# Hybrid encoder with 32 experts on one core: rows of the last four experts kept in SBUF, the rest read back inside the loop

## The chip, the cores and the metric

The kernel runs on one core of a Trainium2 chip, as one launch. The metric is the time of that launch in microseconds; the median of three runs before the change is 1280.09 (1280.09 to 1281.01). The core has TensorE (PE, matmuls into PSUM), VectorE (DVE), ScalarE (ACT), GpSimd (POOL) and SyncE (SP, which here only issues transfers), and 16 DMA engines.

## The reference

Two layers over 512 tokens of 1024 float32 channels. Layer 0 mixes tokens with windowed attention, layer 1 with a gated DeltaNet that runs in both directions. Each ends with a mixture of experts, which is what the change touches:

```python
g_prob, g_idx = lax.top_k(jax.nn.softmax(g_logits, axis=-1), 1)      # 1 of 4 groups
e_prob, e_idx = lax.top_k(jax.nn.softmax(e_sel, axis=-1), TOP_K)     # 2 of its 8 experts
gate = g_prob * e_prob / jnp.sum(e_prob, axis=-1, keepdims=True)
expert_id = g_idx * EXPERTS_PER_GROUP + e_idx
combine = jnp.sum(jax.nn.one_hot(expert_id, N_EXPERTS, dtype=jnp.float32) * gate[..., None], axis=1)
hid = jax.nn.silu(jnp.einsum('td,edf->tef', t, w_gate)) * jnp.einsum('td,edf->tef', t, w_up)
hid = hid * combine[..., None].astype(hid.dtype)
return jnp.einsum('tef,efd->td', hid, w_down).reshape(B, S, D)
```

Every token so has two experts; x = x + (that sum) ends the layer. An expert is three matrices of 1 MB (gate, up: 1024 x 256; down: 256 x 1024), so one layer's 32 experts are 96 MB, read once each.

## The kernel before

Each engine has one instruction stream, written out by hand; semaphores join them. The order within a stream is the order of the code, so an instruction that waits holds up all that follows on its engine. There is no planner.

*Routing.* After the token mixer, `route_pe` and `moe_dve` find each token's two experts and its rank among an expert's tokens (`rank_f`). An expert has 64 slots (SLOTS). `idx_i[:, 0, e]` lists the token of each slot of expert e, `idx_i[:, 1, e]` the row of `y_rows` that each slot's result goes to. Where an expert had more than 64 tokens, `late_passes` would do the rest; every engine tests for it once in a layer, and it was not entered. `pick_rows` makes the rows of experts 0 and 1 with one-hot products; VectorE and ScalarE copy them out of PSUM (L1298, L1213), and the first transpose (`turn`, L1124) follows.

*The expert loop*, for e from 0 to 31. GpSimd gathers the rows of expert e + 4 from `h_rows` (L995). TensorE multiplies them by gate and up (`gate_and_up`, L1132), turns the next expert's rows (L1124), multiplies the hidden rows of expert e - 1 by its down matrix (`down_rows`, L1141, into bank 3: 64 slots x 1024 columns stand as two halves of 128 partitions), and turns the hidden rows of e (L1185). ScalarE computes silu (L1224) and copies turned rows (L1217). VectorE multiplies silu by up (L1323), copies the output of e - 1 to `y_out` (`take_y`, L1319) and the turned hidden rows of e (L1328). GpSimd scatters `y_out` to `y_rows` in DRAM, at row (choice k, token) (`scatter`, L1002).

*Weights.* SP issues the loads of all weights in order (`load_gate_up` L2382, `load_down` L2388) into 7 homes for gate and up and 8 for down, each as soon as TensorE has used its former content. One of these homes is x itself: x is written to `x_rows` before the loop and read again behind the last weights (L2428). For layer 1's token mixer, a first panel of 2 MB (L2373) follows in the same queue.

*The tail of layer 0.* When all scatters have landed, SP reads `y_rows` back as two rows of 1024 for each token (`read_back`, L1392, 8 transfers of 512 KB) into `y_in` in the arena. VectorE, which has meanwhile split the low part of the first panel (`split_low`, L174; ScalarE the high part, L168), adds gate times row to x (`combine_best` L1348, `combine_second` L1353), normalises (`norm_dve`, L285 and L288) and turns; the first projection of the DeltaNet begins on TensorE (`first_unit_half`, L150). Spare matmuls (`spare_pe`, L1092) fill TensorE's time in places.

*The tail of layer 1.* `send_out` reads back in the same way (L1377), `finish_dve` adds (L1363), and each tile of x is stored to the output (L1383).

## Time and profile before

| | us |
|---|---|
| median of 3 runs | 1280.09 |
| the profiled execution | 1278.82 |
| its span on the core | 1277.1 |
| TensorE busy | 1145.1 (90%) |
| VectorE busy | 519.5 (41%) |
| ScalarE busy | 383.5 (30%) |
| GpSimd busy | 385.5 (30%) |
| read from and written to HBM | 265.83 MB and 27.26 MB |

The first expert loop runs from about 251 to 492, the second from about 1012 to 1255. A row of the page cuts the span into 40 slices and gives a digit for each: the busy share in tenths. In a timeline, each line is one or several like instructions: start, length, engine, line of the code, operation, output<-inputs, count, and in brackets how long the engine was idle before it and what ended that. "SPq" is the issuing of transfers, not their run. A row of --windows gives for each engine its busy time and its instructions. A row of a group by form gives busy time and mean ns of one behind the first bar.

### The profile page before, as it was taken

Reading aid. Unit: us, or ns where it says so; the run is one execution under the profiler, and the core shown is the slowest. Engines: PE = TensorE matmul, PEld = TensorE weight load, DVE = VectorE, ACT = ScalarE, POOL = GpSimd, SP = SyncE. Lnnn points to the kernel's source line nnn. Section 1 sums busy time; section 2 is a strip of 40 time slices with the busy share of each in tenths; the row PEclk is TensorE's granted clock in tenths of the full one; section 3 lists DMA queues with packets and bytes.
Section 4 is the critical chain, followed back from the end, with each engine's and each line's share of the span. In section 5 each row is a group of like instructions: output and inputs, shape, how many; then the busy total and the mean of one; then the engine's idle time right before and its main releaser. Section 6 shows DMA issues by size and latency. Waiting matters only on the chain.

```text
span 1277.1 us, 21577 instructions
## 1 busy us (share of the span) xinstructions
PE 1145.1 (90%) x8755; PEld 805.1 (63%) x8755; DVE 519.5 (41%) x1188; ACT 383.5 (30%) x854; POOL 385.5 (30%) x428
## 2 busy tenths in 40 slices
PE   5999999899999884989889999889999899999782
PEld 4876678655555442868568887678888555555441
DVE  4466663411111114564684455753653411111114
ACT  3426841111111102354553445543422111111010
POOL 1233621112232211047545266542301022322110
PEclk9999999999999997989999999999999899999896
DMA  7121047999999998111000120002366999999996
GB/s 241 67 73 67 2 192 277 368 364 381 383 386 379 383 392 320 69 66 67 2 3 1 67 101 31 3 2 81 151 247 261 359 372 389 388 386 377 380 390 247
DMA packets 67795, 278.24 MB, mean 218 GB/s; under 512 B 16888, under 2 KB 16984, under 8 KB 43120
## 3 DMA queue, kind: packets, MB, share of 16 engines
q1 hardware_dynamic: 56480, 255.89, 52.7%
q0 software_dynamic: 11072, 20.43, 4.7%
q8 instruction: 72, 1.18, 0.4%
q10 hardware_dynamic: 144, 0.52, 0.1%
q14 instruction: 27, 0.22, 0.1%
HBM read 265.83 MB, written 27.26 MB: 230 GB/s over the span
## 4 chain that ended last, share of the span: by engine, by line
PE 69%; DMA 13%; DVE 8%; ACT 4%; SPq 3%; issue 2%; POOL 1%; DVEq 0%; POOLq 0%
PE bank L1132 14%; PE bank L150 9%; PE bank L152 8%; PE bank L151 8%; DMA hn<-in_moe_w_up 8%; PE bank L1141 6%; PE bank L1676 4%; PE bank L1124 3%; DMA x<-in_moe_w_up 3%; SPq L2382 2%; PE bank L541 2%; PE bank L550 1%; PE bank L575 1%; PE bank L389 1%; PE bank L298 1%
## 5 line engine op out<-in xcount | busy, mean ns | idle before, releaser
L1002 POOL DMA_INDIRECT y_rows<-arena,idx_i x64 | 64.5, 1008 | 350.0 <-DVE arena L1319 345.0
L1224 ACT ACTIVATE arena<-bank 128x128 f32<-128x128 f32 x64 | 17.7, 277 | 368.2 <-PE bank L1132 368.2
L1323 DVE TENSOR_TENSOR arena<-arena,bank 128x128 f32<-128x128 f32 x64 | 18.4, 287 | 259.2 <-ACT arena L1224 259.2
L152 PE MATMUL bank<-ring_r,ht_r 128*128 128x512 f32 x288 | 113.0, 392 | 0.0
L1132 PE MATMUL bank<-ring,arena 128*64 128x256 f32 x832 | 101.6, 396 | 7.7 <-DMA ring<-in_moe_w_up 6.7
L1319 DVE COPY arena<-bank 128x512 f32<-128x512 f32 x64 | 44.2, 691 | 144.2 <-PE bank L1141 144.2
L150 PE MATMUL bank<-ring_r,arena_r 128*128 128x512 f32 (+1 forms) x228 | 91.3, 401 | 6.1 <-DVE ring_r L174 5.4
L151 PE MATMUL bank<-ring_r,arena_r 128*128 128x512 f32 x224 | 87.8, 392 | 0.0
L1132 PEld LDWEIGHTS bank<-ring,arena 128*64 128x64 f32 x832 | 57.9, 136 | 42.7 <-DMA ring<-in_moe_w_up 7.7
L151 PE MATMUL bank<-ht_r,ring_r 128*128 128x512 f32 (+1 forms) x224 | 80.9, 361 | 0.0
L1124 PEld LDWEIGHTS bank<-ident,arena 64*128 64x128 f32 x512 | 61.3, 201 | 28.3 <-issue 25.1
L995 POOL DMA_INDIRECT arena<-h_rows,idx_i x60 | 57.1, 951 | 66.7 <-issue 36.4
L174 POOL TENSOR_TENSOR ring_r<-ring,ring_r 128x1024 fp32r<-128x1024 f32 x32 | 75.8, 2389 | 2.7 <-ACT ring_r L168 2.7
L2173 DVE SCALAR_TENSOR_TENSOR arena<-bank,arena 128x511 f32<-128x511 f32 (+1 forms) x72 | 53.9, 749 | 51.0 <-ACT arena L1870 49.3
L1124 PE MATMUL bank<-ident,arena 64*128 64x64 f32 x512 | 70.0, 277 | 1.6 <-DVE arena L1298 1.6
L152 PEld LDWEIGHTS bank<-ring_r,ht_r 128*128 128x128 f32 x288 | 54.3, 189 | 11.6
L150 PE MATMUL bank<-ring_r 128*128 128x512 f32 (+1 forms) x144 | 55.8, 387 | 3.3 <-DVE hn L2364 2.0
L168 ACT CAST ring_r<-ring 128x1024 fp32r<-128x1024 f32 x52 | 52.1, 1047 | 9.3 <-DMA ring<-in_gdn_w_in 6.0
L150 PEld LDWEIGHTS bank<-ring_r,arena_r 128*128 128x128 f32 (+1 forms) x228 | 42.9, 188 | 17.8 <-ACT arena_r L305 4.9
L1217 ACT COPY arena<-bank 128x512 f32<-128x512 f32 x64 | 37.4, 585 | 48.2 <-PE bank L1124 48.2
L1132 PE MATMUL bank<-arena 128*64 128x256 f32 x320 | 43.2, 427 | 6.3 <-DMA arena<-in_moe_w_up 4.8
L1676 PE MATMUL bank<-arena,ring 128*128 128x128 f32 x352 | 45.6, 291 | 3.6 <-POOL ring L2049 2.9
(343 smaller groups left out, 2338.4 us busy)
## 6 DMA issues: line engine op xcount, KB each, us to landing
ring<-in_moe_w_gate SPq DMA_DIRECT2D x26, 1024.0 KB, 21.5
ring<-in_moe_w_up SPq DMA_DIRECT2D x26, 1024.0 KB, 25.3
arena<-in_moe_w_down SPq DMA_DIRECT2D x24, 1024.0 KB, 27.5
ring<-in_moe_w_down SPq DMA_DIRECT2D x24, 1024.0 KB, 26.9
ring<-in_gdn_w_in SPq DMA_DIRECT2D x8, 2048.0 KB, 8.0
arena<-in_moe_w_gate SPq DMA_DIRECT2D x10, 1024.0 KB, 19.4
arena<-in_moe_w_up SPq DMA_DIRECT2D x10, 1024.0 KB, 23.3
ht<-in_moe_w_gate SPq DMA_DIRECT2D x10, 1024.0 KB, 27.0
```

The costliest lines, as they stand in the source:

```text
L150: pe.matmul(dst, a[0], b[0], start=start, stop=False)
L151: pe.matmul(dst, a[0], b[1], start=False, stop=False)
L152: return pe.matmul(dst, a[1], b[0], start=False, stop=stop)
L168: act.copy(panel(n, True, True)[:, c, :], panel(n)[:, c, :]).then_inc(panel_high, 1)
L174: eng.tensor_tensor(panel(n, False, True)[:, c, :], panel(n)[:, c, :], panel(n, True, True)[:, c, :].bitcast(F32), ALU.subtract).then_inc( ...
L995: pool.indirect_dma_start(out=rows_of(e), out_offset=None, in_=h_rows[l], in_offset=bass.IndirectOffsetOnAxis(ap=idx_i[0:SLOTS, 0, e:e + 1 ...
L1002: pool.indirect_dma_start(out=y_rows[l], out_offset=bass.IndirectOffsetOnAxis(ap=idx_i[:, 1, e:e + 1], axis=0), in_=y_out[:, e % RING, :], ...
L1124: last = pe.transpose(bank[0][:, c * SLOTS:(c + 1) * SLOTS], rows_of(e)[:, c::KC], ident[at, at])
L1132: last = pe.matmul(bank[1][m * SLOTS:(m + 1) * SLOTS, 0:2 * P].rearrange("p (w n) -> p w n", w=2), xgt[:, i, c * SLOTS:(c + 1) * SLOTS], w ...
L1141: last = pe.matmul(bank[3][half * SLOTS:(half + 1) * SLOTS, :], hidden_t[:, i, m * SLOTS:(m + 1) * SLOTS], d[:, m, half * HALF:(half + 1) ...
L1676: last = pe.matmul(bank[b][:, h * P:(h + 1) * P], lhs(h), rhs(h), start=True, stop=True)
L2173: last = dve.scalar_tensor_tensor(out=acc, in0=bank[U % 4][:, of], scalar=tap(k, unit), in1=acc, op0=ALU.mult, op1=ALU.add)
```

## The change

The outputs of experts 28 to 31 (`SENT` to 31) are not scattered. VectorE multiplies them by the slot's gate while it takes them out of PSUM (`keep_y`), two experts to a pair of 128-partition tiles, odd experts with their halves changed over. ScalarE and VectorE split each into a rounded high part and a low part (`kept_high`, `kept_low`). Where a token's row stands in a pair is marked by one-hot matrices (`mark_slots`, `turn_marks`, `spread_of`), and TensorE adds the rows of both pairs for each half tile of 512 columns in one PSUM bank (`kept_pair`), which VectorE adds to x (`add_kept_dve`). The gates of the slots come from eight small products ahead of the loop (`gates_to_slots`); the operations that compute the gates move ahead of the loop's first copy.

The other rows are still scattered and read back. The read-back stands behind the x tiles in SP's stream and waits for expert 28's output. Its homes are the down homes 1 to 4. Tiles 0 and 1 are added by VectorE, tile 0 between experts 30 and 31 and behind expert 31, tile 1 behind the loop; tiles 2 and 3 are scaled by ScalarE (`scale_rows`) and added by GpSimd. Both layers now have the same tail. Rows of `y_rows` that no one writes any more are multiplied by a gate of 0; so that they hold numbers, both `y_rows` are filled with x during the attention (`fill_rows`, 16 writes). The second panel of the DeltaNet's projection waits for all additions, and TensorE for all of x.

Left out below: the places of new buffers and counts of semaphores, the late passes (which are not entered), and the small operations on gates.

```diff
+KEPT = 4
+SENT = EXPERTS - KEPT
...
-        y_in = [cut(2 * D * t, 2, D) for t in range(TT)]
+        y_in = [dn_home[1 + t].rearrange("p (k n) -> p k n", k=2) for t in range(TT)]
+        y_late = [gu_home[4 + t // 2][:, t % 2 * 2 * D:(t % 2 + 1) * 2 * D].rearrange("p (k n) -> p k n", k=2)
+                  for t in range(TT)]
...
+            for e in range(SENT):
                 if e + AHEAD < EXPERTS:
                     gather(e + AHEAD)
                 scatter(e)
+            pool.wait_ge(x_again, Y_FILLED + 16 * TT * (l + 1))
+            for t in (2, 3):
+                for k in range(2):
+                    pool.wait_ge(s["exp_g"], 6 + 2 * (t - 2) + k + l * PER["exp_g"])
+                    last = pool.tensor_tensor(x[:, t, :], x[:, t, :], y_in[t][:, k, :], ALU.add)
+                    if k == 0 or t == 2:
+                        o.step(last)
+            last.then_inc(s["idx"], 1)
...
-            def down_rows(i, slot):
+            def down_rows(i, slot, turned_halves=0):
                 d = down(slot)
                 for m in range(FC):
                     for half in range(2):
-                        last = pe.matmul(bank[3][half * SLOTS:(half + 1) * SLOTS, :],
+                        side = half ^ turned_halves
...
+            def gates_to_slots():
+                pe.wait_ge(s["onehots"], 2 + l * PER["onehots"])
+                for n in range(2 * TT):
+                    last = pe.matmul(bank[2][:, 2 * EXPERTS:2 * EXPERTS + KEPT], at_slot[:, n // TT, n % TT, :],
+                                     last_gate[:, n, :], start=n == 0, stop=n == 2 * TT - 1)
+                last.then_inc(s["ranks"], 1)
+
+            def turn_marks():
+                pe.wait_ge(s["onehots"], 3 + l * PER["onehots"])
+                for q in range(2):
+                    for ab in range(2):
+                        for t in range(TT):
+                            last = pe.matmul(bank[4 + 2 * q + ab][:, t * P:(t + 1) * P],
+                                             marks_of(q, t)[:, ab * SLOTS:ab * SLOTS + P], unit_r,
+                                             start=True, stop=True)
+                        last.then_inc(s["ranks"], 1)
+
+            def kept_pair(q, n):
+                t, ab = n // 2, n % 2
+                for high in (True, False):
+                    if n < 2:
+                        if high:
+                            pe.wait_ge(s["exp_e"], 2 + 2 * q + ab + l * PER["exp_e"])
+                        else:
+                            pe.wait_ge(s["dve"], 3 + 2 * q + ab + l * PER["dve"])
+                    last = pe.matmul(bank[(4 + n) % 8][:, :], spread_of(q, ab)[:, t * P:(t + 1) * P],
+                                     kept_y(q, ab, high), start=q == 0 and high, stop=q == 1 and not high)
+                return last
+
+            def add_kept():
+                pe.wait_ge(s["exp_g"], 5 + l * PER["exp_g"])
+                pe.wait_ge(s["xgt"], EXPERTS * (l + 1))
+                pe.wait_ge(s["hidden"], EXPERTS * (l + 1))
+                pe.wait_ge(s["hid_t"], EXPERTS * (l + 1))
+                for n in range(2 * TT - 1):
+                    kept_pair(0, n)
+                pe.wait_ge(s["y_copied"], EXPERTS * (l + 1))
+                kept_pair(0, 2 * TT - 1)
+                for n in range(2 * TT):
+                    kept_pair(1, n).then_inc(s["lists"], 1)
...
+            gates_to_slots()
             turn(0)
             for e in range(EXPERTS):
                 body(e)
+                if e == SENT - 1:
+                    turn_marks()
             project_down(EXPERTS - 1)
             late_passes(pe, l, None, late)
+            add_kept()
...
+            def scale_rows(t):
+                act.wait_ge(y_back[t], 16 + 32 * (l + 1))
+                for k in range(2):
+                    act.activation(y_in[t][:, k, :], y_in[t][:, k, :], ACT.Copy, scale=stat[:, 10 + k, t:t + 1]
+                                   ).then_inc(s["exp_g"], 1)
+
+            def kept_high(q):
+                act.wait_ge(s["placed"], 2 * TT + 1 + q + l * PER["placed"])
+                act.copy(kept_y(q, 0, True), kept_y(q, 0, False, False)).then_inc(s["exp_e"], 1)
+                act.wait_ge(s["y_copied"], SENT + 2 * q + 2 + l * PER["y_copied"])
+                act.copy(kept_y(q, 1, True), kept_y(q, 1, False, False)).then_inc(s["exp_e"], 1)
...
+                if e == SENT:
+                    for n in range(4):
+                        act.wait_ge(s["ranks"], 3 + n + l * PER["ranks"])
+                        act.copy(spread_of(n // 2, n % 2), bank[4 + n][:, :]).then_inc(s["exp_g"], 1)
+                if e == SENT + 2:
+                    kept_high(0)
+            scale_rows(2)
+            kept_high(1)
+            scale_rows(3)
...
+            def keep_y(e):
+                q, odd_one = (e - SENT) // 2, e % 2
+                dve.wait_ge(s["y_sum"], e + 1 + l * PER["y_sum"])
+                for ab in range(2):
+                    at = slice(SLOTS * (ab ^ odd_one), SLOTS * ((ab ^ odd_one) + 1))
+                    last = dve.tensor_scalar(kept_y(q, ab, False, False)[at, :], bank[3][at, :],
+                                             slot_gate[at, e - SENT:e - SENT + 1], None, ALU.mult)
+                    if odd_one and ab == 0:
+                        last.then_inc(s["placed"], 1)
+                last.then_inc(s["y_copied"], 1)
+
+            def kept_low(q):
+                for ab in range(2):
+                    dve.wait_ge(s["exp_e"], 2 + 2 * q + ab + l * PER["exp_e"])
+                    dve.tensor_tensor(kept_y(q, ab, False), kept_y(q, ab, False, False),
+                                      kept_y(q, ab, True).bitcast(F32), ALU.subtract).then_inc(s["dve"], 1)
+
+            def mark_slots():
+                numbers = slot_no[:, 0:SLOTS].unsqueeze(1).unsqueeze(1)
+                for q in range(2):
+                    marks = flat_ring[True][:, 2 * PAIR + q * 3 * TT * SLOTS:2 * PAIR + (q + 1) * 3 * TT * SLOTS]
+                    marks = marks.rearrange("p (t w n) -> p t w n", t=TT, w=3)
+                    for w, n in ((0, 2), (2, 1)):
+                        first = 2 * q + w % 2
+                        dve.tensor_tensor(marks[:, :, w:w + n, :], numbers.to_broadcast([P, TT, n, SLOTS]),
+                                          last_slot[:, :, first:first + n].unsqueeze(3).to_broadcast([P, TT, n, SLOTS]),
+                                          ALU.is_equal)
+                dve.tensor_copy(unit_r, ident[:, :]).then_inc(s["onehots"], 1)
...
+                if e > SENT:
+                    keep_y(e - 1)
+                elif e:
                     take_y(e - 1)
                 dve.wait_ge(s["hid_turned"], e + 1 + l * PER["hid_turned"])
                 dve.tensor_copy(hidden_t[:, e % RING, :], bank[2][:, 0:P]).then_inc(s["hid_t"], 1)
-            take_y(EXPERTS - 1)
+                if e == SENT - 2:
+                    mark_slots()
+                if e == SENT + 2:
+                    kept_low(0)
+                    combine_rows(dve, l, 0, 0, o)
+                if e == SENT + 3:
+                    combine_rows(dve, l, 0, 1, o)
+            keep_y(EXPERTS - 1)
+            kept_low(1)
...
+            combine_rows(dve, l, 1, 0, o)
+            combine_rows(dve, l, 1, 1, o)
+            for t in range(TT):
+                add_kept_dve(dve, l, t)
...
+        def combine_rows(dve, l, t, k, o):
+            if k == 0:
+                dve.wait_ge(x_again, Y_FILLED + 16 * TT * (l + 1))
+                dve.wait_ge(y_back[t], 16 + 32 * (l + 1))
+            o.step(dve.scalar_tensor_tensor(out=x[:, t, :], in0=y_in[t][:, k, :], scalar=stat[:, 10 + k, t:t + 1],
+                                            in1=x[:, t, :], op0=ALU.mult, op1=ALU.add))
+
+        def add_kept_dve(dve, l, t):
+            if t == 2:
+                dve.wait_ge(s["idx"], 2 + l * PER["idx"])
+            for half in range(2):
+                n = 2 * t + half
+                c = slice(half * HALF, (half + 1) * HALF)
+                dve.wait_ge(s["lists"], 2 + n + l * PER["lists"])
+                dve.tensor_tensor(x[:, t, c], bank[(4 + n) % 8][:, :], x[:, t, c], ALU.add
+                                  ).then_inc(s["combined"], 1)
...
+        def fill_rows(sp):
+            for l in range(2):
+                whole = y_rows[l].rearrange("(r h) n -> r (h n)", h=2)
+                for n in range(2 * TT):
+                    sp.dma_start(whole[n * P:(n + 1) * P, :], x[:, n % TT, :]).then_inc(x_again, 16)
...
+            sp.wait_ge(s["ranks"], PER["ranks"] * (l + 1))
+            sp.wait_ge(s["y_sum"], SENT + 1 + l * PER["y_sum"])
...
+            read_back(sp, l)
...
+            fill_rows(sp)
...
-            used = [(s["up"], 27), (s["y_sum"], 32)] + [(g["proj"], 4), (g["proj"], 8), (g["av"], 8), (g["proj"], 16)]
+            used = [(s["up"], 27), (s["combined"], 2 * TT)] + [(g["proj"], 4), (g["proj"], 8), (g["av"], 8), (g["proj"], 16)]
...
-                if i == 0:
-                    read_back(sp, 0)
...
+            pe.wait_ge(s["combined"], 2 * TT)
...
-            for t in range(2):
-                combine_best(dve, t, o)
-                combine_second(dve, t)
```

## Rows read from the trace of the kernel before

**Rows 1.** The page, the span in 40 slices of 31.9 us.

```profile
...
DMA  7121047999999998111000120002366999999996
...
```

**Rows 2.** Timeline, end of the first expert loop (start, length, engine, line, [idle before]).

```profile
...
483.60 3.85 PE L1132 MATMUL bank<-hn,arena 128*64 128x256 f32 x32 [0.82 <-DMA hn<-in_moe_w_up]
...
487.80 0.29 DVE L1323 TENSOR_TENSOR arena<-arena,bank 128x128 f32<-128x128 f32 x1 [4.35 <-ACT arena L1224]
...
490.20 1.94 PE L1141 MATMUL bank<-arena 128*64 128x512 f32 x8 [0.78 <-DVE arena L1328]
...
498.55 3.88 ACT L168 CAST ring_r<-ring 128x1024 fp32r<-128x1024 f32 x4 [5.97 <-DMA ring<-in_gdn_w_in]
...
499.62 4.63 DVE L174 TENSOR_TENSOR ring_r<-ring,ring_r 128x1024 fp32r<-128x1024 f32 x4 [5.90 <-ACT ring_r L168]
...
506.82 4.76 PE L1092 MATMUL bank<-router,ones 128*128 128x288 f32 x12 [14.69 <-DVE x L1353]
...
510.05 0.15 DVE L285 TENSOR_SCALAR norm_s<-norm_s 128x1 f32<-128x1 f32 x1
...
518.15 0.36 PE L150 MATMUL bank<-ring_r 128*128 128x256 f32 x1 [1.30 <-DVE ht_r L318]
...
```

**Rows 3.** One line's instruction and landing: last x tile read again, first layer.

```profile
...
L2428 SPq DMA_DIRECT2D x<-x_rows x1: 6911/6911/6911, 467.6 to 467.6; - x1
...
DMA to landing us min/median/max: 25.0/25.0/25.0
```

**Rows 4.** The same for the last x tile of the second layer.

```profile
...
L2428 SPq DMA_DIRECT2D x<-x_rows x1: 2762/2762/2762, 1230.8 to 1230.8; - x1
...
DMA to landing us min/median/max: 23.4/23.4/23.4
```

**Rows 5.** Windows (PE, PEld, DVE, ACT, POOL busy; granted clock; DMA share; GB/s).

```profile
...
496.00:498.00 2.00, 0.00 (x0) 0.00 (x0) 0.00 (x0) 0.00 (x0) 0.00 (x0) 0.60 0.16 64
508.00:510.00 2.00, 2.00 (x6) 1.43 (x5) 1.96 (x2) 0.00 (x0) 0.00 (x0) 0.50 1.03 414
510.00:512.00 2.00, 1.59 (x7) 0.92 (x5) 1.32 (x3) 1.15 (x2) 0.56 (x1) 0.99 1.02 398
...
```

**Rows 6.** Timeline, last expert and tail of the second layer.

```profile
...
1246.17 3.85 PE L1132 MATMUL bank<-hn,arena 128*64 128x256 f32 x32 [0.93 <-DMA hn<-in_moe_w_up]
...
1250.38 0.29 DVE L1323 TENSOR_TENSOR arena<-arena,bank 128x128 f32<-128x128 f32 x1 [4.46 <-ACT arena L1224]
...
1252.77 1.94 PE L1141 MATMUL bank<-arena 128*64 128x512 f32 x8 [0.78 <-DVE arena L1328]
...
1262.44 10.26 DVE L1363 SCALAR_TENSOR_TENSOR x<-arena,x 128x1024 f32<-128x1024 f32 x9 [7.00 <-DMA arena<-y_rows]
1268.86 4.66 SPq L1383 DMA_DIRECT2D out<-x  x5
```

**Rows 7.** Timeline, start of the first expert loop.

```profile
...
240.93 1.90 PE L1117 MATMUL bank<-arena 128*128 128x64 f32 x16
...
250.76 0.69 DVE L1298 COPY arena<-bank 128x512 f32<-128x512 f32 x1 [7.48 <-PE bank L1152]
...
251.50 0.76 PE L1124 MATMUL bank<-ident,arena 64*128 64x64 f32 x5 [0.79 <-DVE arena L1298]
...
```

**Rows 8.** Groups by form on VectorE: costs of one operation.

```profile
...
L1363 DVE SCALAR_TENSOR_TENSOR x<-arena,x 128x1024 f32<-128x1024 f32 x7 | 8.8, 1284 | 7.1 <-DMA arena<-y_rows 7.0
...
L406 DVE TENSOR_TENSOR x<-x,bank 128x512 f32<-128x512 f32 x16 | 11.0, 687 | 40.0 <-PE bank L152 40.0
...
```

**Rows 9.** Groups by form on ScalarE.

```profile
...
L1217 ACT COPY arena<-bank 128x512 f32<-128x512 f32 x64 | 37.4, 585 | 48.2 <-PE bank L1124 48.2
...
L271 ACT ACTIVATE hn<-x 128x1024 f32<-128x1024 f32 x16 | 16.9, 1058 | 87.7 <-DVE x L406 72.3 <-DVE x L1353 11.0 <-DMA x<-in_x 4.1
...
```

**Rows 10.** Groups by form on GpSimd.

```profile
...
L174 POOL TENSOR_TENSOR ring_r<-ring,ring_r 128x1024 fp32r<-128x1024 f32 x32 | 75.8, 2389 | 2.7 <-ACT ring_r L168 2.7
...
L2121 POOL TENSOR_TENSOR ring<-arena 128x512 f32<-128x512 f32 x12 | 12.2, 1039 | 2.0 <-PE bank L1676 2.0
...
```

140 lines of the change are left out of this document (80 added, 60 removed).

## The prediction

> **What bounds the kernel now.** I read the DMA row of the page first: its share is 9 tenths or more through both expert loops and near zero in most of what lies before each [rows 1]. Read next to it the timeline at the end of the first loop: the last expert's gate and up product began at 483.60, when its weights landed, and that expert's output left TensorE at 492.14 (490.20 + 1.94). From there to 518.15, the first projection of the next layer, TensorE has no matmul that the output needs: 26.0 us for scattering, reading back, adding and normalising [rows 2]. So the loops end by DMA, and behind each is a tail in which VectorE and transfers take turns.
>
> The landings say when a transfer queued in the loop arrives. The last of the four x tiles read again was issued at 467.6 and landed 25.0 us later, at 492.6 [rows 3]; in the second layer at 1230.8 + 23.4 = 1254.2 [rows 4]. That is after the last expert's weights in both. The windows give the rate of plain 4 KB rows, 414 GB/s, so 1 MB of two row tiles takes 2.5 us and 4 MB 10.1 us; they also give TensorE's granted clock: idle since 492.14, it shows a mean of 0.60 in 496 to 498 and 0.50 (the 1.2 GHz level) in 508 to 510, although it works from 506.82; the next row has 0.99 [rows 5]. In the second layer the last product began at 1246.17, its hidden product ran at 1250.38, its output was done at 1254.71; the last output store was issued from 1268.86 on and the span ended at 1277.1 [rows 6].
>
> **The change, part by part.** All sums are against the profiled execution, 1278.82 us with a span of 1277.1; the median of the runs is 1280.09, 1.27 more, which I add at the end.
>
> *Fill of y_rows.* 16 writes of 512 KB, 8.4 MB, 20 us at 414 GB/s, are issued on SP behind the second attn_w_out load, issued at about 105. The DMA row is at zero in slices 5 of 128 to 160 us and nearly so around it, and SP's next load of expert weights waits until the attention ends [rows 1]. Price 0; without that cover 20 us.
>
> *Start of the expert loop.* Eight one-hot products with 4 columns stand between the picking of rows and the first transpose. The nearest row is the same number with 64 columns, 1.90 us; bounds 1.0 (weights alone, my estimate as half of it) and 1.9, I take 1.6. They begin when the picking ends, about 250.7, so the transpose begins at 252.3, not 251.50: +0.8. The some 16 small VectorE operations moved ahead fit in its 7.48 us of idle time there [rows 7]. TensorE frees the weight homes, so the loads shift with it, and DMA ends the loop: +0.8 in each layer, +1.6 in all (0 to 2.2).
>
> *In the loop.* The marks, their 16 transposes, four copies, and a second VectorE instruction for each kept tile (0.69 each, the price of 512 columns out of PSUM [rows 8]) meet one to three microseconds of waiting for weights per expert, as the 0.82 before 483.60. Price 0 up to expert 30. Four scatters fewer save only what lies ahead of the last weights, below 0.3 us.
>
> *The read-back moved inside.* This is the step that decides. SP asks for it once expert 28's output is there (about 474 and 1237), behind the x tiles in the same queue. VectorE waits for the first tile and for all four x tiles between experts 30 and 31, in its own stream. Behind that wait stand the hidden product of expert 31, the keeping of expert 30, the copy of the turned hidden rows; TensorE's last transpose and last down product wait for these, and ScalarE's splitting of the last pair waits in turn behind its own wait for tile 2. First tile in the first layer: between 492.6 (landed with x) and 495.1 (one tile behind), I take 494.0. Then:
>
> VectorE adds the first half of tile 0 (1.28 [rows 8], with its wait 1.3) to 495.3; hidden product to 495.6, against 487.8 before. Keeping expert 30 and the copy (2 x 0.65 + 0.3) to 497.2. TensorE has then been idle since its products of about 489.2, as it was from 492.14 ahead of the low row [rows 5], so I take the lower clock: the last down product costs 3.9 instead of 1.94, to 501.2. Keeping expert 31, to 502.6. ScalarE: tile 2 lands at 499.0, its two scalings (1.06 each) end at 501.1, the two roundings (0.59 each [rows 9]) at 503.2. The low part to 503.9, the test for late passes 0.4, tile 1's two additions to 506.9. The one-hot products, 32 of 512 columns at 0.24 (eight passes in 1.94), run ahead of that, from 501.6 to 509.3. VectorE then takes eight half tiles out of PSUM at 0.61 from start to start (0.69 long): 511.8. GpSimd's four additions: 1024 columns cost 2.39 in one row and 2 x 1.04 in another [rows 10]; at 2.1 from 500.1 they end at 508.5, just ahead of VectorE's need at 509.3.
>
> Now comes what VectorE formerly did while it waited: the low split of the first projection panel, 4.63 from 499.62, and 0.42 for the gate weights. The panel is itself queued behind 4 MB: formerly landed at 498.55, now 508.6 if all 10.1 us come on top, and some 504.9 (my estimate) if part of it fits into DMA share that lay idle before (0.16 was busy in 496 to 498, which alone gives 1.7); I take 506.6, which ScalarE's split turns into 507.6. So VectorE goes on to 516.9. From its first normalising instruction to the first projection took 8.1 us (510.05 to 518.15); the addition in the middle is gone, I take 7.6: 524.5. First layer: +6.3. Its bounds: with the early landings and the higher clock 521.1, +3.0; with the late ones and 2.39 on GpSimd 525.9, +7.8. TensorE's work behind that point is unbroken before and stays so.
>
> Second layer by the same steps: first tile between 1254.2 less what idle DMA share gives (1252) and 1256.7, I take 1255.5; hidden product to 1257.1 against 1250.7; last output, at the lower clock, 1262.7; kept 1264.1, split 1265.4, tile 1 1268.4, eight additions 1273.4. The end follows 4.4 behind the last addition (1262.44 + 10.26 = 1272.7, span end 1277.1 [rows 6]): 1277.8, +0.7. Bounds: -4.7 and +2.3.
>
> *Taken away.* Of 8 additions of 1024 columns behind each read-back two stay on VectorE behind the loop; 10.26 us become 2.6 + 4.9 [rows 6]. That gain is real, but it begins 8 and 6 us late.
>
> *Waits moved.* The second panel of the projection now waits for all additions (about 512 instead of 503) and lands near 520; it was split only from 538 on. TensorE's wait for all of x rather than for its first tile costs nothing: normalising is behind it anyway.
>
> Sum: 1.6 + 6.3 + 0.7 = +8.6: 1287.4 profiled, **1288.7** as a median. With every lower bound: 0 + 3.0 - 4.7 = -1.7, 1278.4; with every upper one 2.2 + 7.8 + 2.3 = +12.3, 1292.4.
>
> *A rule against the change.* The additions of tile 1 on VectorE read two operands of SBUF while GpSimd's do too. GpSimd's same-sized additions are 2.39 in one row and 2.08 in another, so some mutual hindrance is possible [rows 10]. The Trainium skill, SBUF — State Buffer, section "SBUF: two separate sides", says that the two share a port pair as "an exclusive lock, not a bandwidth split", for a VectorE operation with two SBUF inputs against a GpSimd one that reads SBUF. By that rule the forecast gains the price of the third rival below; without it the sum above stands. No row here shows the two engines' additions of this size side by side.
>
> *Order of landings.* The x tiles landed 25.0 and 23.4 us after their issue, behind weights issued before them [rows 3, 4]. The Trainium skill, DMA: Bandwidth & Descriptors, section "Queues, rings and completion order", says that descriptors of one issuing engine are consumed in ring order on each DMA engine, but that completion is not first in, first out. The first half speaks for the wait; the second allows single tiles to land early, which is the first rival.
>
> **Rivals.**
> 1. *The rows are there in time* (faster). One mechanism: the first tile lands before 487.5 and 1250.1, VectorE never waits, the clock holds. Then the second tail is 1254.7, kept 1256.1, split 1257.9, tile 1 1260.9, additions 1265.8, end 1270.3: -6.8. The first tail gains nothing: the panel behind 4 MB lands at 504.9 at the earliest, and 1.05 + 4.65 + 7.6 is 518.2. Sum -6.8 + 1.6: 1274.9 as a median. For it: transfers queued in one stream do not land in strict order. Against: the x tiles alone, waited for at the same place, landed at 492.6 and 1254.2.
> 2. *Landings at the lower bounds* (no change): the idle share of the DMA engines takes the read-back, the clock stays up: -1.7 to +1, some 1279.8. For it: the DMA share had fallen below 1 before the loop's end.
> 3. *GpSimd and VectorE exclude each other*: each of two additions of tile 1 waits up to 2.1 for GpSimd, whose last then ends 2.6 later; 2.6 to 4.2 in each layer on top of the sum, 1294.5.
> 4. *The change does not do what it says*: the rows are asked for inside the loop and arrive behind it. That is the forecast's own mechanism.
>
> **How the numbers follow.** Forecast 0.58, rival 1 0.12, rival 2 0.18, rival 3 0.12. The range takes in rival 2 and the upper bound: 1279 to 1294. What a measurement can tell is 0.2%, 2.6 us. Slower: the forecast, rival 3 and a small part of rival 2 make 0.71; rival 2's rest and the forecast's low edge 0.15; faster 0.14.
>
> **What would show it.** In the profile after: the hidden product of expert 31 idle until a read-back tile or x lands, some 6 to 8 us past the end of its gate and up product; TensorE's clock at 0.5 in the last down product; VectorE's low split of the panel behind the additions, the first projection 5 to 7 us later relative to the last weights; the first transpose about 1 us later. I am wrong if VectorE finds tile 0 landed, or if the first projection starts no later than before.

## The result, and the profile after

| | before | after |
|---|---|---|
| median of the runs, us | 1280.55 (4 runs, 1280.09 to 1281.83) | 1300.74 (4 runs, 1297.96 to 1302.20) |
| ratio, 95% interval | | 1.0153 (1.0133 to 1.0174) |
| the profiled execution, its span | 1278.82, 1277.1 | 1302.20, 1300.2 |

Slower, as forecast, but by 20 us instead of 8.6: the time is above the range of 1279 to 1294. The profiled execution is the slowest of the four, about 1.5 above their median; I come to that below.

I cut both spans at the same instructions: the last gate and up product of each layer, the first projection between them, and the end.

| stretch | before | after | difference | forecast |
|---|---|---|---|---|
| start to last gate and up product, layer 0 | 483.6 | 484.5 | +0.9 | +0.8 |
| from there to the first projection (first tail) | 34.6 | 47.6 | +13.1 | +6.3 |
| from there to the last gate and up product, layer 1 | 728.0 | 730.6 | +2.6 | +0.8 |
| from there to the end (second tail) | 30.9 | 37.4 | +6.5 | +0.7 |
| sum | | | +23.1 | +8.6 |

First tail in the profile after, by the timeline (start, length, engine, line); the rows answer to [rows 2].

```profile
...
484.50 3.85 PE L1172 MATMUL bank<-hn,arena 128*64 128x256 f32 x32 [0.44 <-DMA hn<-in_moe_w_up]
...
495.99 1.28 DVE L1528 SCALAR_TENSOR_TENSOR x<-ring,arena,x 128x1024 f32<-128x1024 f32 x1 [9.22 <-DMA ring<-y_rows]
497.31 0.29 DVE L1478 TENSOR_TENSOR arena<-arena,bank 128x128 f32<-128x128 f32 x1
...
497.66 0.47 PE L1226 MATMUL bank<-ident,arena 128*128 128x128 f32 x1 [7.60 <-DVE arena L1478]
...
499.45 3.68 PE L1182 MATMUL bank<-arena 128*64 128x512 f32 x8 [1.32 <-DVE arena L1485]
...
500.98 2.19 ACT L1308 ACTIVATE arena<-arena 128x1024 f32<-128x1024 f32 x2 [12.31 <-DMA arena<-y_rows]
...
502.27 5.37 POOL L1045 TENSOR_TENSOR x<-x,arena 128x1024 f32<-128x1024 f32 x2 [33.29 <-ACT arena L1308]
...
503.24 1.53 DVE L1452 TENSOR_SCALAR ring<-bank,slot_gate 64x512 f32<-64x512 f32 x2 [2.58 <-PE bank L1182]
...
504.69 3.50 DVE L1461 TENSOR_TENSOR ring_r<-ring,ring_r 128x512 fp32r<-128x512 f32 x2
...
507.72 6.02 POOL L1045 TENSOR_TENSOR x<-x,ring 128x1024 f32<-128x1024 f32 x2
508.12 6.71 DVE L1528 SCALAR_TENSOR_TENSOR x<-spare,arena,x 128x1024 f32<-128x1024 f32 x2
508.64 3.89 ACT L170 CAST ring_r<-ring 128x1024 fp32r<-128x1024 f32 x4 [0.83 <-DMA ring<-in_gdn_w_in]
514.86 4.88 DVE L1538 TENSOR_TENSOR x<-bank,x 128x512 f32<-128x512 f32 x8
...
519.99 4.62 DVE L176 TENSOR_TENSOR ring_r<-ring,ring_r 128x1024 fp32r<-128x1024 f32 x4
...
```

Read it from the top. VectorE stood 9.22 us until the second row of tile 0 had landed, and the hidden product of expert 31 (L1478) came at 497.31 instead of 487.80: the forecast's wait. TensorE had no work for 7.60 us, and the last down product took 3.68 instead of 1.94. Then look at the pairs that overlap: the two low parts (L1461), 0.68 each when alone, took 3.50 beside GpSimd's addition, and the two additions of tile 1 (L1528), 1.28 each when alone, 6.71. The eight additions out of PSUM (L1538) took what was forecast, 4.88.

The second tail, from the last hidden product on, answers to [rows 6].

```profile
...
1272.81 1.28 DVE L1528 SCALAR_TENSOR_TENSOR x<-ring,arena,x 128x1024 f32<-128x1024 f32 x1 [7.80 <-DMA ring<-y_rows]
...
1276.27 3.68 PE L1182 MATMUL bank<-arena 128*64 128x512 f32 x8 [1.32 <-DVE arena L1485]
...
1279.00 4.86 POOL L1045 TENSOR_TENSOR x<-x,arena 128x1024 f32<-128x1024 f32 x2 [30.99 <-ACT arena L1308]
...
1281.51 5.66 DVE L1461 TENSOR_TENSOR ring_r<-ring,ring_r 128x512 fp32r<-128x512 f32 x2
...
1283.94 5.46 POOL L1045 TENSOR_TENSOR x<-x,ring 128x1024 f32<-128x1024 f32 x2
...
1287.09 4.71 DVE L1528 SCALAR_TENSOR_TENSOR x<-spare,arena,x 128x1024 f32<-128x1024 f32 x2
...
1291.84 4.87 DVE L1538 TENSOR_TENSOR x<-bank,x 128x512 f32<-128x512 f32 x8
...
```

Here the low parts took 5.66 and tile 1's additions 4.71. The page after, in 40 slices of 32.5 us, has this DMA row for the one in [rows 1]: the fill is the 7 and 1 in slices 4 and 5, the rest is nearly the same.

```profile
...
DMA  7127157899999995111000121002366999999993
...
```

The start of the loop answers to [rows 7]: the gates' products took 1.84, against 1.6 forecast, and the transpose follows at 253.60. That is 2.1 later than before, not 0.8, because the picking ahead of it ended later in this execution (251.8 against 250.7); at the last gate and up product 0.9 of it was left.

```profile
...
251.83 1.84 PE L1231 MATMUL bank<-arena 128*128 128x4 f32 x16
...
253.60 1.09 PE L1164 MATMUL bank<-ident,arena 64*128 64x64 f32 x8
...
```

### The profile page after: what moved, and what is told of

Its sections match the earlier page's. It is cut to its first block, busy times and chain, and to the rows that moved or that the text cites. A ratio compares the mean times of both kernels' runs of the same rounds, so it can differ in the third digit from the quotient of the medians.

```text
span 1300.2 us, 21938 instructions
## 1 busy us (share of the span) xinstructions
PE 1176.4 (90%) x8883; PEld 830.3 (64%) x8883; DVE 550.3 (42%) x1243; ACT 400.7 (31%) x878; POOL 399.6 (31%) x428
## 4 chain that ended last, share of the span: by engine, by line
PE 67%; DMA 14%; DVE 9%; ACT 4%; SPq 3%; issue 2%; POOL 1%; DVEq 0%
PE bank L1172 12%; PE bank L152 9%; PE bank L154 8%; PE bank L153 8%; DMA ring<-in_moe_w_up 8%; PE bank L1182 6%; PE bank L1847 4%; PE bank L1164 3%; DMA ring<-y_rows 3%; DMA arena<-in_moe_w_up 2%; PE bank L546 2%; PE bank L555 1%; PE bank L580 1%; PE bank L300 1%; PE bank L392 1%
## 5 line engine op out<-in xcount | busy, mean ns | idle before, releaser
L1028 POOL DMA_INDIRECT y_rows<-arena,idx_i x56 | 57.2, 1021 | 301.6 <-DVE arena L1445 295.5
L1478 DVE TENSOR_TENSOR arena<-arena,bank 128x128 f32<-128x128 f32 x64 | 18.4, 288 | 243.0 <-ACT arena L1322 242.9
L1445 DVE COPY arena<-bank 128x512 f32<-128x512 f32 x56 | 38.7, 692 | 128.6 <-PE bank L1182 128.6
L154 PEld LDWEIGHTS bank<-ring_r,ht_r 128*128 128x128 f32 x288 | 54.6, 190 | 11.7
L152 PEld LDWEIGHTS bank<-ring_r,arena_r 128*128 128x128 f32 (+1 forms) x228 | 43.1, 189 | 17.1 <-ACT arena_r L307 4.9
L1303 ACT COPY arena<-bank 128x512 f32<-128x512 f32 x64 | 37.4, 585 | 49.9 <-PE bank L1164 49.9
L1182 PE MATMUL bank<-arena 128*64 128x512 f32 x192 | 50.0, 644 | 2.6 <-DVE arena L1485 2.6
L1226 PEld LDWEIGHTS bank<-ident,arena 128*128 128x128 f32 x64 | 9.0, 140 | 64.3 <-issue 48.7
```

What stands on the lines that cost most here:

```text
L152: pe.matmul(dst, a[0], b[0], start=start, stop=False)
L154: return pe.matmul(dst, a[1], b[0], start=False, stop=stop)
L1028: pool.indirect_dma_start(out=y_rows[l], out_offset=bass.IndirectOffsetOnAxis(ap=idx_i[:, 1, e:e + 1], axis=0), in_=y_out[:, e % RING, :], ...
L1182: last = pe.matmul(bank[3][side * SLOTS:(side + 1) * SLOTS, :], hidden_t[:, i, m * SLOTS:(m + 1) * SLOTS], d[:, m, half * HALF:(half + 1) ...
```

## The experiments

All times are medians; the kernel before was measured beside each (1279.7 to 1280.4) and ratios are against it. After is 1300.7.

### What GpSimd's additions cost

**In the kernel before, by itself.** Four additions of 1024 columns on GpSimd, read by nobody, beside VectorE's in the second tail:

```diff
...
             moe_pool(pool, 1, o)
+            pool.wait_ge(y_sent[0], Y_SENT[0] + 16)
+            for t in range(TT):
+                pool.tensor_tensor(hn[:, t, :], y_in[0][:, 0, :], y_in[0][:, 0, :], ALU.add)
```

> The kernel before, with four additions of 1024 columns on GpSimd (2.1 to 2.4 us each when alone), started when the first tile of the second layer has been read back, that is beside VectorE's eight of 1.28 us; their result is read by nobody. It measures by itself what GpSimd's additions do to VectorE's. Theory A (only one of the two engines has the port when both read two operands of SBUF): VectorE's additions beside them take up to 3.4 us, and the end comes 4 to 9 us later. Theory B (they share it with little loss): VectorE's stay at 1.28 to 1.6, the end comes under 1.5 us later, and what was slow in the kernel after has another cause.

Measured: 1283.94, ratio 1.0039 (1.0022 to 1.0056); span 1282.4 against 1277.1. First VectorE's groups by form while GpSimd worked (until 1272.6), then those behind it:

```profile
...
L1363 DVE SCALAR_TENSOR_TENSOR x<-arena,x 128x1024 f32<-128x1024 f32 x4 | 11.4, 2920 | 6.9 <-DMA arena<-y_rows 6.9
...
L1363 DVE SCALAR_TENSOR_TENSOR x<-arena,x 128x1024 f32<-128x1024 f32 x3 | 3.7, 1279 | 0.0
...
L2527 POOL TENSOR_TENSOR hn<-arena 128x1024 f32<-128x1024 f32 x4 | 10.4, 2625 | 5.1 <-DMA arena<-y_rows 5.1
...
```

The same operation took 2.92 us beside GpSimd's additions and 1.28 without them, four times in a row, one for each of GpSimd's. The engines take turns, a pair every 2.83 us. Theory A, by the lengths. The last addition ends 6.0 later (1278.73, formerly 1272.69) and the span is 5.3 longer; the median moved by 3.6 (2.8 to 7.2 by the interval), just under theory A's 4 and clear of theory B's 1.5.

**In the kernel after.** First in both layers:

```diff
-                    last = pool.tensor_tensor(x[:, t, :], x[:, t, :], y_in[t][:, k, :], ALU.add)
+                    last = pool.tensor_tensor(x[:, t, 0:32], x[:, t, 0:32], y_in[t][:, k, 0:32], ALU.add)
```

> The kernel after, with GpSimd's four additions of 1024 columns cut to 32 columns each: 992 of 1024 columns of the read-back rows of tiles 2 and 3 are left out of the result, and nothing else. The wait inside the loop and the slow last down product stay. VectorE's operations that took 0.68 and 1.28 us alone and up to 2.9 and 3.4 beside GpSimd's additions then have nothing beside them. Theory A (GpSimd's additions cost what the forecast missed): the last addition out of PSUM comes 6 us earlier in each layer (L0 at about 513.5 instead of 519.7, L1 6.5 earlier), and the time is 1300.7 - 12.5 = 1288, within 2 of the forecast of 1288.7. Theory B (the additions out of PSUM wait for the one-hot products or for the rows, whatever GpSimd does): under 6 us in all, 1295 or more.

Measured: 7487.59. The routing of the second layer hangs on the first layer's rows; an expert then had more than 64 tokens and the late passes ran, so this time says nothing. But the first tail of its trace lies ahead of that routing, and it is the first tail of the kernel after without GpSimd's additions:

```profile
...
504.56 1.46 DVE L1461 TENSOR_TENSOR ring_r<-ring,ring_r 128x512 fp32r<-128x512 f32 x2
506.91 2.61 DVE L1528 SCALAR_TENSOR_TENSOR x<-spare,arena,x 128x1024 f32<-128x1024 f32 x2 [0.90 <-issue]
509.55 4.87 DVE L1538 TENSOR_TENSOR x<-bank,x 128x512 f32<-128x512 f32 x8
...
526.80 0.36 PE L152 MATMUL bank<-ring_r 128*128 128x256 f32 x1 [0.79 <-DVE ht_r L320]
...
```

1.46 and 2.61 in place of 3.50 and 6.71. The last addition ends at 514.42, 5.3 earlier than in the kernel after (theory A had 6), and the tail, from the last gate and up product at 484.33 to the first projection, is 42.5, 5.1 shorter than after's 47.6. The wait for tile 0 (8.79 us) and the slow last product (3.68) are still in it.

With 32 columns in the second layer alone (`n = 32 if l else D`):

> The kernel after, with GpSimd's four additions cut to 32 of their 1024 columns in the second layer only, where no routing hangs on them: 992 of 1024 columns of the read-back rows of tiles 2 and 3 are left out of the second layer's result. The wait in the loop and the slow last down product stay, the first layer is whole. Theory A (GpSimd's additions cost what the forecast missed): in the second tail the two low parts and tile 1's additions take 0.68 and 1.28 us each instead of 2.89, 2.84 and 3.39, the last addition comes 6 to 6.5 us earlier relative to the last gate and up product (27.5 instead of 33.9 behind it), the tail from there to the end is 31 instead of 37.4, and the time 1294.5. Theory B (the additions out of PSUM wait for the one-hot products or for the rows, whatever GpSimd does): under 3 us, 1298 or more.

Measured: 1294.65, ratio 1.0116 (1.0085 to 1.0147). The second tail is 31.4 (1260.1 to 1291.5), 6.0 shorter than after's 37.4. VectorE in its timeline:

```profile
...
1278.88 1.45 DVE L1462 TENSOR_TENSOR ring_r<-ring,ring_r 128x512 fp32r<-128x512 f32 x2
1280.57 2.60 DVE L1529 SCALAR_TENSOR_TENSOR x<-spare,arena,x 128x1024 f32<-128x1024 f32 x2 [0.24 <-issue]
1283.21 4.87 DVE L1539 TENSOR_TENSOR x<-bank,x 128x512 f32<-128x512 f32 x8
...
```

1.45 and 2.60 in place of 5.66 and 4.71. The wait in the loop and the slow last product are still in this kernel, and its second tail of 31.4 is what I had forecast (31.6). So the second layer's miss is GpSimd's additions, shown; and of the first layer's 6.8 they are 5.1, by the trace above.

**GpSimd's share given to VectorE.** Tiles 2 and 3 added by VectorE; the scaling on ScalarE and GpSimd's additions are gone, and with them the waits for them (the cut shows ScalarE's and VectorE's streams):

```diff
...
-            scale_rows(2)
             kept_high(1)
-            scale_rows(3)
...
             combine_rows(dve, l, 1, 1, o)
+            for t in (2, 3):
+                combine_rows(dve, l, t, 0, o)
+                combine_rows(dve, l, t, 1, o)
```

> The changed kernel, but VectorE adds all four tiles itself; ScalarE scales nothing and GpSimd adds nothing; VectorE's wait inside the loop stays. Theory A (VectorE operations with two SBUF operands are blocked while GpSimd adds): the two low parts of the last pair take 1.3 us together instead of 3.5 and 5.7, the two additions of tile 1 take 2.6 instead of 6.7 and 4.7; what is saved pays for the four additions more on VectorE, 5.1 us: -2 us in all against the changed kernel. Theory B (these rows are long for another reason, the transfers that write SBUF or waits inside them): they stay as long, and the four additions come on top, +5 us in each layer, +10.

Measured: 1298.79, ratio 1.0146 (1.0110 to 1.0183); the first tail is as long as after's (47.7), the second 36.7 against 37.4. The low parts took 1.45 and tile 1's additions 2.61, as theory A had it. The medians are 2.0 apart, but the runs overlap (1298.36 to 1300.13 here, 1297.96 to 1302.20 after), so no difference can be told: four more additions of 1.30 in each layer on VectorE cost about what the turns with GpSimd did, and GpSimd's help gained nothing that these runs can tell.

### What the wait in the loop costs

**The wait moved behind the loop, nothing else.**

```diff
...
                     kept_low(0)
-                    combine_rows(dve, l, 0, 0, o)
-                if e == SENT + 3:
-                    combine_rows(dve, l, 0, 1, o)
...
             kept_low(1)
+            combine_rows(dve, l, 0, 0, o)
+            combine_rows(dve, l, 0, 1, o)
```

> The changed kernel, but VectorE adds tile 0 behind the loop, not between experts 30 and 31 and behind 31. Theory A (VectorE's wait for the first tile is what makes the tails late, as the prediction had it): the last down product ends some 9 us earlier in each layer and both tails end 7 to 8 us earlier, together -15 us against the changed kernel. Theory B (ScalarE, which waits for tile 2 ahead of its rounding of the last pair, holds the tail as late by itself): the last down product is 9 us earlier, but the low part of the last pair follows the landing of tile 2 and moves by 1 to 2 us in each layer, together -3 us.

Measured: 1306.23, ratio 1.0210 (1.0173 to 1.0248): 5.5 slower than after, no run of the one within the range of the other. Both theories expected a gain, and both fell. The expert's last output left TensorE at 492.2 instead of 503.1, and yet:

```profile
...
501.95 4.25 DVE L1461 TENSOR_TENSOR ring_r<-ring,ring_r 128x512 fp32r<-128x512 f32 x2 [8.15 <-ACT ring_r L1313]
506.13 6.72 DVE L1527 SCALAR_TENSOR_TENSOR x<-ring,arena,x 128x1024 f32<-128x1024 f32 x2
514.44 2.60 DVE L1527 SCALAR_TENSOR_TENSOR x<-spare,arena,x 128x1024 f32<-128x1024 f32 x2 [1.59 <-issue]
...
```

The low parts wait 8.15 us for ScalarE's rounding, which stands in its stream behind the wait for tile 2; the wait was only handed on. And tile 0's additions, which after made while it was waiting anyway, now stand behind the loop, beside GpSimd's.

**The same, with ScalarE's rounding ahead of its wait** (`kept_high(1)` before `scale_rows(2)`):

> The changed kernel without VectorE's wait inside the loop and with ScalarE rounding the last pair ahead of its wait for tile 2; GpSimd still adds tiles 2 and 3. Theory B of e1 (two waits, either of which holds the tail) gives -12 us against the changed kernel, some 9 more than e1. If VectorE's wait alone were the cause, the same as e1. If GpSimd's additions are themselves the longer chain (four of 2.1 to 2.4 from tile 2's landing on), the additions of tiles 2 and 3 wait for them by 5 us.

Measured: 1292.45, ratio 1.0093 (1.0060 to 1.0126), 8.3 below after; 12 was expected. VectorE:

```profile
...
496.93 1.45 DVE L1461 TENSOR_TENSOR ring_r<-ring,ring_r 128x512 fp32r<-128x512 f32 x2
...
502.49 4.60 DVE L1527 SCALAR_TENSOR_TENSOR x<-spare,arena,x 128x1024 f32<-128x1024 f32 x2 [1.59 <-issue]
503.66 5.64 POOL L1045 TENSOR_TENSOR x<-x,arena 128x1024 f32<-128x1024 f32 x2 [32.30 <-ACT arena L1308]
...
507.12 2.48 DVE L1537 TENSOR_TENSOR x<-bank,x 128x512 f32<-128x512 f32 x4
...
```

Two things in it: one of tile 1's additions still waits for GpSimd (4.60 for two), and the four additions out of PSUM from 507.12 on, beside GpSimd's, which lasted until 509.30, took 2.48, no more than alone. So only the operations with two inputs in SBUF waited for GpSimd.

**Both undone**: no wait in the loop, all additions on VectorE.

> Both edits together: no VectorE wait inside the loop, all additions on VectorE, ScalarE rounds the last pair at once. If wait and blocking are the causes: additions end near 512 in the first layer and near 1290 less the shift of the first layer in the second, -7 and -6.5 us, together -14 us against the changed kernel, so still 6 us slower than before. If the wait is not a cause: as e2.

Measured: 1290.21, ratio 1.0080 (1.0049 to 1.0110), 10.5 below after; 14 was expected, and the tails (41.7 and 32.2) are 5.9 and 5.2 shorter, not 7 and 6.5. With GpSimd's additions, in the experiment before this one, they are 43.1 and 33.3. Against the kernel with all additions on VectorE (1298.79) the wait in the loop is worth 8.6, without GpSimd in the picture. What is left of the tails is VectorE's work: in the second, from 1269.35 to 1288.55 with one gap of 1.0 us.

**The clock.** Twelve matmuls read by nobody while VectorE waits:

```diff
...
                     project_down(e - 1)
+                if e == EXPERTS - 1:
+                    pe.wait_ge(s["exp_g"], 5 + l * PER["exp_g"])
+                    spare_pe(pe, 12, 4)
```

> The kernel after, with 12 matmuls whose output nobody reads put on TensorE between experts 30 and 31, as soon as the spread matrices are copied, so that TensorE is not idle while VectorE waits for the read-back. After: the last down product took 3.68 us in both layers, behind 7.60 and 6.16 us without a matmul; before it took 1.94. Theory A (the idle time lowers the clock, and the last product is on the path): the product takes 1.9 to 2.7 us, the two tails are 1 to 1.7 us shorter each, some 2 to 3.4 us in all against the kernel after (1300.7). Theory B (the slow product is covered by ScalarE's rounding, which in the first layer waits for tile 2 until 501.3 anyway): the product is faster and the first tail stays; under 1.7 us in all. If the matmuls end long before the wait does, the product stays at 3.68 and the run tells nothing.

Measured: 1299.63, ratio 1.0157 (1.0136 to 1.0179). The stretch of the last down product by windows (busy by engine, granted clock, DMA share, GB/s), after and then here:

```profile
...
499.40:503.10 3.70, 3.65 (x9) 0.90 (x9) 1.26 (x1) 2.12 (x2) 0.83 (x1) 0.50 0.81 319
1276.20:1279.90 3.70, 3.63 (x9) 0.88 (x9) 1.28 (x1) 2.19 (x2) 0.90 (x1) 0.50 0.22 89
...
```

```profile
...
499.10:501.10 2.00, 1.95 (x9) 0.65 (x9) 1.27 (x1) 0.41 (x1) 0.00 (x0) 1.00 0.81 320
1273.30:1275.30 2.00, 1.91 (x9) 0.61 (x9) 1.28 (x1) 0.50 (x1) 0.00 (x0) 1.00 0.38 150
...
```

0.50 (the 1.2 GHz level) became 1.00 (2.4 GHz) and the product 1.94 us in both layers, but the tails are 47.4 and 37.0, against 47.6 and 37.4. The median is 1.1 below after's, within its spread. Theory B: the product was slow because TensorE had stood idle before it, as forecast, and it did not set the end. The low parts and additions behind it fell beside GpSimd's, and those start with tile 2's landing, not with the product (4.29 for the two low parts in the first tail; 3.39 and 3.28 for tile 1's additions in the second).

### What is left

**Order of the first tail.** As both undone, and the rows of tiles 2 and 3 added behind the normalising of tiles 0 and 1, as the kernel before did; TensorE then waits for tiles 0 and 1 alone:

```diff
...
             combine_rows(dve, l, 1, 1, o)
-            for t in (2, 3):
-                combine_rows(dve, l, t, 0, o)
-                combine_rows(dve, l, t, 1, o)
-            for t in range(TT):
-                add_kept_dve(dve, l, t)
+            if l:
+                for t in (2, 3):
+                    combine_rows(dve, l, t, 0, o)
+                    combine_rows(dve, l, t, 1, o)
+            for t in range(TT) if l else (0, 2, 3, 1):
+                add_kept_dve(dve, l, t, o)
...
             norm_dve(dve, 2, 1)
+            combine_later(dve, 2, 0, o)
             turn_dve(dve, 3, 0)
             turn_dve(dve, 3, 1)
+            combine_later(dve, 2, 1, o)
+            combine_later(dve, 3, 0, o)
+            combine_later(dve, 3, 1, o)
```

> The kernel with no wait in the loop and all additions on VectorE (1290.2 measured), and in the first layer the additions of the rows of tiles 2 and 3 moved behind the normalising of tiles 0 and 1, as the kernel before had it. That takes four additions of 1.28 us from the path to the first projection. Theory A (the rest of the first tail is VectorE's queue of work, nothing else): the first projection begins 4 to 5 us earlier, at 520.5 to 521.5 instead of 525.3, and the time is 1285 to 1286.5. Theory B (the second operand decides: the first projection panel, which lands at 507.6 behind the rows read back): it is no more than 1 to 2 us earlier.

Measured: 1286.10, ratio 1.0057 (1.0034 to 1.0079); the first projection at 521.28, where it was expected. It is the best form of the change that I found, and still 5.7 above before; its tails are 37.8 and 32.2 against 34.6 and 30.9.

**A plain delay.** Six additions of VectorE ahead of the normalising, in the kernel before:

```diff
...
+            dve.wait_ge(s["combined"], 2)
+            for _ in range(6):
+                o.step(dve.tensor_tensor(hn[:, 3, :], x[:, 0, :], x[:, 1, :], ALU.add))
             norm_dve(dve, 2, 0)
```

> The kernel before, with six idle additions of 1024 columns on VectorE (6 x 1.28 = 7.7 us) ahead of the normalising in the first layer's tail, written where nobody reads. It asks what a delay there is worth at the end. Theory A (all of what follows is shifted): 1280 + 7.7 = 1287.7, +7 to +8.5. Theory B (the delay shifts the places at which TensorE's granted clock falls and rises in the mixer that follows, and this adds or gives back some us, as the 7.1 us later projection of the last variant that became 14.2 us at the second loop): +10 to +15, or below +5, and the granted clock by stretch differs between the two.

Measured: 1285.44, ratio 1.0045 (1.0026 to 1.0064). VectorE's delay was 7.53 and the first tail became 42.5 (+7.9); the median moved by 5.1, the interval allows 3.3 to 8.2. That lies between theory A (7 to 8.5) and theory B (over 10 or under 5). A delay in this tail reaches the end for the most part (the profiled execution: 5.5 at the end, after a loop that ended 1.6 earlier); whether in full, the interval does not say.

**The start.** The gates' products twice in each layer (`gates_to_slots(False)` ahead of the first):

> The kernel after, with the eight one-hot products of 4 columns that carry the gates to the slots done twice ahead of the first transpose of each expert loop. They took 1.84 us once. Theory A (the loop's start sets all that follows, as TensorE frees the homes of the weights): the first transpose 1.84 us later and the end 1.8 later per layer, +3.7 in all. Theory B (the weights already wait in SBUF and the DMA engines end the loop; a late start is caught up): the first gate and up product is later by 1.8 us, the last one by under 0.5, and the time moves by under 1 us.

Measured: 1305.10, ratio 1.0197 (1.0181 to 1.0213), 4.4 above after, 3.7 expected. What stands ahead of the first transpose reaches the end.

**The fill.** The 16 writes done twice (`for l in (0, 1, 0, 1)`, each eight behind the landing of those before):

> The kernel after, with the 8.4 MB that fill the expert rows in DRAM written twice, the second time behind the first. The first fill was issued from 105.8 us on and had landed by 135.1. Theory A (nothing else needs the DMA engines or SP there): the second lands by about 165 and the time does not move, within 1 us. Theory B (SP's later loads or the first expert's weights come late): the first expert loop begins later, by up to the 20 to 29 us that a fill takes.

Measured: 1300.59, ratio 1.0160 (1.0144 to 1.0177). The last of the 32 landed at 164.2, SP's next load was issued at 175.5. Theory A: the median is 0.15 from after's.

**The token mixer between.** From the first projection to the first gate and up product of layer 1 the traces show 496.3 before, 501.1 after, 503.3 with both undone, and 496.6 to 499.0 in the ten others that did not run the late passes, the delayed one among them. TensorE does nearly the same work there, so I looked at the clock: windows of 20 us on TensorE (busy, granted clock, DMA share, GB/s), first after, then the kernel with the spare matmuls, whose projection begins 0.5 us earlier.

```profile
...
630.00:650.00 20.00, 15.10 (x207) 1.00 0.00 1
650.00:670.00 20.00, 16.54 (x402) 0.91 0.01 2
...
```

```profile
...
630.00:650.00 20.00, 14.25 (x199) 1.00 0.00 1
650.00:670.00 20.00, 17.29 (x460) 1.00 0.01 3
...
```

At about the same place the clock was 0.91 in the one execution and 1.00 in the other. The spans of after's four runs spread from 1295.9 to 1300.2, and the profiled one is the longest. Of the +2.6 in the table, +4.8 lies in the mixer and -2.1 in the second loop; beyond the 0.8 of the second start I read it as this spread, which is not shown. What makes the clock dip in one execution and not in another is open, and so is whether the dips make up the whole spread.

## Why the prediction was wrong

*Right.* DMA ends the loops; the start's price passes through (done twice it cost 4.4 more, 3.7 expected; the single +0.9 for 0.8 is weaker evidence, since the last gate and up product of the first layer came anywhere from 482.8 to 486.0 in ten traces with the same start); the fill is free; VectorE's wait for tile 0, its place and its release; the late hidden product and the low clock; the panel landing at 508.6 (its upper bound); additions out of PSUM at 0.61 from start to start; the second panel (asked for at 519.8, landed at 527.6) never in the way. The first tail from its last addition to the projection was forecast as 12.7 and took 12.4.

*The step that failed* is "The low part to 503.9, the test for late passes 0.4, tile 1's two additions to 506.9", with its twin "split 1265.4, tile 1 1268.4". I priced four VectorE operations as if alone while I had GpSimd adding from 500.1 on. The mechanism was written down, as rival 3 with a chance of 0.12, but mis-sized too: 2.6 to 4.2 a layer, for tile 1's additions alone. Measured: low parts 3.50 and 5.66 instead of 1.45, tile 1's additions 6.71 and 4.71 instead of 2.60, that is 6.2 more in the first tail and 6.3 in the second.

On the forecast's own chain part of that was hidden: from the end of keeping expert 31 to the end of tile 1's additions it had 4.3 in each tail, and 10.1 and 10.2 were measured, 5.8 and 5.9 more. The tails missed the forecast by 6.8 and 5.8. The rest leaves 1.0 in the first tail and cancels in the second: the keeping itself ended 1.3 and 0.9 late, for the most part because tile 0 came late, and the stretches behind the last addition were 0.3 and 0.9 shorter. The experiments show the cause in both tails: without GpSimd's additions the second is 6.0 shorter and the first 5.1.

The rows to see it were there. GpSimd's additions of 2.39 and 2.08 per 1024 columns [rows 10] did not tell, but in the token mixer of the kernel before, beside GpSimd's split of a panel, a VectorE operation of only 64 columns with both inputs in SBUF took 2.42 us, while one of 512 columns with an input in PSUM kept its 0.69:

```profile
...
548.18 4.74 POOL L174 TENSOR_TENSOR ring_r<-ring,ring_r 128x1024 fp32r<-128x1024 f32 x2
...
548.25 0.69 DVE L2236 TENSOR_TENSOR arena<-bank,arena 128x512 f32<-128x512 f32 x1 [1.51 <-POOL arena L2034]
...
550.57 2.42 DVE L2141 SCALAR_TENSOR_TENSOR arena<-arena 128x64 f32<-128x64 f32 x1
...
```

Here the Trainium skill, SBUF — State Buffer, section "SBUF: two separate sides", was right and the forecast gave it too little: whoever of the two starts first keeps the port pair for the whole instruction, and of VectorE's operations here it concerns those with two inputs in SBUF. The traces agree on who is held: 1.28 became 2.92 four times out of four, and four additions with one input in PSUM kept their 2.48. They do not bear out "the whole instruction" for the recorded length: a pair took 2.83 us, less than the 1.28 and 2.36 that the two take alone. Priced by what the chain then measured, the forecast would have been 8.6 + 11.7 = 20.3, 1300.4 as a median; that this is within 0.4 of the measured median is partly luck, with a mixer that varies by 7 us between traces.

*Smaller misses.* The first tile was ready at 495.9 instead of 494.0, since the wait is for both of its rows: about 1 us in the first tail beyond the 0.9 by which the loop itself was later. The low clock on the last product, which I counted at 1.96 in each tail, is real and cost 0.2 to 0.4 in this kernel. The forecast had ScalarE's rounding behind the rows of tile 2 (to 503.2), but not that this wait holds the tail as late by itself; the first experiment of the wait showed it. Of the signs that I gave, the hidden product came 9.0 and 7.5 us behind the end of its gate and up product (6 to 8 said), the first projection 13.1 later (5 to 7), the first transpose 2.1 later (about 1).

*Readings and sums.* TensorE did have needed work between 492.14 and 518.15: two groups of eight transposes of normalised rows, 1.16 us each, at 512.23 and 514.24. The 495.6 of the hidden product is its end and the 487.8 beside it a start. Rival 3's own price gives 1293.9 to 1297.1, not one 1294.5, and its upper part lies outside the range.

*Rivals.* Rivals 1 and 2 fell: no tile was there in time. Rival 3's mechanism held on top of the forecast, at 1.5 to 2.4 times its size; even its upper price would have left the median 3.6 above.

*Why the change loses even at its best.* It removes VectorE's idle time behind the loop, 7.00 us in the second tail [rows 6] and 5.90 in the first [rows 2], and fills it with VectorE's work. Second tail, both undone: the rest of the last output's keeping 1.53, two low parts 1.45, eight additions of rows 10.4, eight out of PSUM 4.88, gaps: 19.2 from TensorE's last output to the last addition; the kernel before needed 18.0 with the transfer in it (1254.71 to 1272.7) [rows 6].

## What to carry to other kernels

Before giving GpSimd a share of VectorE's work, list what VectorE does in the same microseconds and mark each operation with two inputs in SBUF: each of them can wait out one GpSimd instruction, and here the help gained nothing while VectorE's side had such operations. An early transfer gains only what its waiting time was not already used for, and a wait taken from one engine's stream must be looked for in the next one's. A clock that was low for one product cost next to nothing here, because that product's output was not what the tail waited for.

## What the runs showed of the hardware

- VectorE's two-input SBUF operation of 128 x 1024 took 2.92 us (mean of four) beside GpSimd additions of the same size and 1.28 alone; at 128 x 512 up to 2.89, and 0.68 alone. GpSimd's own went from 2.36 to as much as 3.2. A pair of one of each took 2.83.
- GpSimd waits too: its additions of 32 columns took 0.25 us alone and 1.17 and 1.24 beside VectorE's two additions of tile 1 (the kernel after with GpSimd's additions cut in the second layer).
- Four VectorE additions with one input in PSUM beside the same GpSimd additions: 2.48 for four, unchanged.
- TensorE without work for 7.60 and 6.16 us: 3.68 us for eight matmuls at a granted clock of 0.50; with twelve spare matmuls in between 1.94 at 1.00.
- Eight read-backs of 512 KB in one queue did not land in the order of issue: in the kernel after the second, issued at 478.0, landed at 495.9, and the third, issued at 480.1, at 494.2.
